# Keys and queries stored as transposed, split columns by the projection stage, in a retention and stick-breaking attention kernel

## The reference, cut to what matters

```python
def shared_kv(x, kv_norm_g, w_kv, sb_k_g):
    kv = rmsnorm(x, kv_norm_g) @ w_kv
    k, v = jnp.split(kv, 2, axis=-1)
    k = rmsnorm(k.reshape(B, L, SB_HEADS, SB_DH), sb_k_g)
    ...
def sb_layer(...):
    q, g = jnp.split(h @ w_in, 2, axis=-1)
    q = rmsnorm(q.reshape(B, L, SB_HEADS, SB_DH), q_g)
    o = stick_breaking(q, k_all, v_all, pos, k_pos, bias).reshape(B, L, SB_W)
    return (jax.nn.silu(g) * o) @ w_out
    ...
# stick_breaking, for query t and key s < t:
#   z[t,s]    = q_t . k_s / sqrt(d) + bias_h
#   A[t,s]    = sigmoid(z[t,s]) * prod_{s<j<t} (1 - sigmoid(z[t,j]))
#   out_t     = sum_s A[t,s] v_s
```

## Time and profile before

| | us |
|---|---|
| runs | 1870.95, 1868.4, 1874.94 |
| median | 1870.95 |
| profiled execution, span | 1868.5 (27997 instructions) |
| retention, up to about | 987 |
| projections of the second layer | 987 to 1352 |
| attention | 1354 to 1760 |
| output product | 1760 to 1868.5 |

### The profile page before, as it was taken

The page is one execution under the profiler, slowest core; times in us unless marked ns, Lnnn a source line. Parts: engine busy times, 40 slices in busy tenths (PEclk is TensorE's granted clock), DMA queues, the critical chain, the costliest instruction groups (busy, mean ns, idle before and its releaser), DMA issues. The chain is left out here.

```text
span 1868.5 us, 27997 instructions
## 1 busy us (share of the span) xinstructions
PE 1801.2 (96%) x10103; PEld 1424.3 (76%) x10103; DVE 1054.1 (56%) x1975; ACT 809.0 (43%) x1682; POOL 81.0 (4%) x140
## 2 busy tenths in 40 slices
PE   4999999999999999999999999999999998999998
PEld 2678787878787878777778777888777777777677
DVE  4653535353635353633656345765168789989752
ACT  3742323232323232412345223533267678989620
POOL 2000000000000000000000000001100000000000
PEclk9999999999999999999999999999999999999999
DMA  9221212131313040583434563212342335554252
GB/s 327 85 94 58 94 58 93 58 94 56 98 52 116 35 128 22 196 275 80 136 79 169 189 217 128 83 67 89 115 113 69 94 94 175 151 150 145 61 176 96
DMA packets 184939, 215.54 MB, mean 115 GB/s; under 512 B 45352, under 2 KB 142560, under 8 KB 183809
## 3 DMA queue, kind: packets, MB, share of 16 engines
q1 hardware_dynamic: 171146, 167.17, 29.2%
q0 software_dynamic: 13696, 47.08, 6.6%
HBM read 165.39 MB, written 48.83 MB: 115 GB/s over the span
## 5 line engine op out<-in xcount | busy, mean ns | idle before, releaser
L475 PE MATMUL rt_acc<-rt_w_hi,rt_h_hi 128*128 128x512 f32 x504 | 203.3, 403 | 1.0 <-DVE rt_h_lo L1017 1.0
L477 PE MATMUL rt_acc<-rt_w_hi,rt_h_lo 128*128 128x512 f32 x504 | 197.1, 391 | 0.0
L476 PE MATMUL rt_acc<-rt_w_lo,rt_h_hi 128*128 128x512 f32 x504 | 196.5, 390 | 0.0
L1060 DVE TENSOR_TENSOR rt_by_cos<-rt_raw,rt_cos 128x256 f32<-128x256 f32 (+1 forms) x72 | 30.5, 424 | 243.8 <-ACT rt_raw L890 243.8
L901 ACT COPY rt_qk_t<-rt_tr 128x256 f32<-128x256 f32 (+1 forms) x72 | 26.0, 361 | 278.6 <-PE rt_tr L709 278.6
L2956 PE MATMUL kq_acc<-kq_w_hi,kq_h 128*128 128x512 f32 x320 | 127.1, 397 | 0.0
L2957 PE MATMUL kq_acc<-kq_w_lo,kq_h 128*128 128x512 f32 x320 | 124.8, 390 | 0.0
L2959 PE MATMUL kq_acc<-kq_w_hi,kq_h 128*128 128x512 f32 x320 | 124.7, 390 | 0.0
L477 PEld LDWEIGHTS rt_acc<-rt_w_hi,rt_h_lo 128*128 128x128 f32 x504 | 94.6, 188 | 20.6
L475 PEld LDWEIGHTS rt_acc<-rt_w_hi,rt_h_hi 128*128 128x128 f32 x504 | 94.9, 188 | 19.2 <-DVE rt_h_lo L1017 1.4
L476 PEld LDWEIGHTS rt_acc<-rt_w_lo,rt_h_hi 128*128 128x128 f32 x504 | 94.9, 188 | 17.9 <-issue 0.2
(11 more groups left out here) (414 smaller groups left out, 4160.1 us busy)
## 6 DMA issues: line engine op xcount, KB each, us to landing
ro_a_raw<-retained SPq DMA_DIRECT2D x14, 1024.0 KB, 5.9
op_ada<-in_ada_w SPq DMA_DIRECT2D x8, 1024.0 KB, 12.8
rt_w_raw<-in_ret_w_in SPq DMA_DIRECT2D x16, 512.0 KB, 5.1
rt_w_raw<-in_ret_w_in SPq DMA_DIRECT2D x8, 1024.0 KB, 7.7
rt_old<-in_state_ret SPq DMA_DIRECT2D x8, 1024.0 KB, 6.0
rt_g_raw<-in_ret_w_in SPq DMA_DIRECT2D x8, 1024.0 KB, 5.2
out_st_sample<-rt_new POOLq DMA_DIRECT2D x8, 1024.0 KB, 8.0
kq_w_raw<-in_sb_w_in SPq DMA_DIRECT2D x4, 2048.0 KB, 8.9
```

The lines of the kernel that those rows point to most:

```text
L475: nc.tensor.matmul(dst, h_hi[:, k, cols], w_hi[:, k, :], start=k == 0, stop=False)
L476: nc.tensor.matmul(dst, h_hi[:, k, cols], w_lo[:, k, :], start=False, stop=False)
L477: last = nc.tensor.matmul(dst, h_lo[:, k, cols], w_hi[:, k, :], start=False, stop=k == KD - 1)
```

## The change

The projection stage transposes the normed rows itself. Behind the product of step s PE turns the four blocks of `kq_out` of step s-1 into a free bank of `kq_tr` (bank 3 in key chunks, bank 1 in query chunks); ACT copies the rounded part and DVE the remainder into `parts` (one buffer, laid over the gate tensor's first half), and POOL stores both, 128 partitions of four runs of 512 bytes each, into new scratch tensors `k_cols` and `q_cols`. Key rows are still stored, as they are outputs; query rows of the prompt are not. Attention loads for each pair both parts of keys and queries for all 1024 positions (`load_heads`, twelve loads of 64 partitions with 4096 bytes each) into buffers of two, and all splits, transposes and copies of keys and queries go from it, with their slots. Sample tiles are treated as before. The page and new-row transposes of the samples take the slots that are free now.

```diff
         self.shift = sb("shift", [P, 3, KD, NC])
+        gate_at = nc.sbuf_base
         self.gate = sb("gate", [NC, 2, D])
+        self.parts = nc.alloc_sbuf_tensor_at("kq_parts", [P, 2, NB // P, P], F32R, offset=gate_at)
         self.cond_t = sb("cond_t", [P, KD, NC])
...
+        self.k_cols = nc.dram_tensor("k_cols", (2, D, SEQ), F32, kind="Internal").ap()
+        self.q_cols = nc.dram_tensor("q_cols", (2, D, SEQ), F32, kind="Internal").ap()
...
-        self.k2 = sb("k2", [P, NPT, 2 * DH])
-        self.k_parts = sb("k_parts", [P, 2, NPT, 2, DH], F32R)
-        self.g_out = sb("g_out", [P, 2, NB])
+        self.k_t = sb("k_t0", [P, 2, SEQ], F32R)
+        self.q_hi = sb("q_hi0", [P, 2, SEQ], F32R)
...
-        self.q4 = sb("q4", [P, 3, 4, 2, 2, DH])
+        self.q_lo = sb("q_lo0", [P, 2, SEQ], F32R)
+        self.g_out = sb("g_out", [P, 2, NB])
...
+HEAD_LOADS = 12
+
+
+def load_heads(sp, ps, pair, k_t, q_hi, q_lo, signal):
+
+    for hh in range(2):
+        cols = slice((2 * pair + hh) * DH, (2 * pair + hh + 1) * DH)
+        for part in range(2):
+            half = slice(part * DH, (part + 1) * DH)
+            sp.dma_start(k_t[half, hh, :].bitcast(F32), ps.k_cols[part, cols, :]).then_inc(signal, 16)
+            sp.dma_start(q_hi[half, hh, :].bitcast(F32), ps.q_cols[0, cols, :]).then_inc(signal, 16)
+            sp.dma_start(q_lo[half, hh, :].bitcast(F32), ps.q_cols[1, cols, :]).then_inc(signal, 16)
 
...
-        k_t = sb("k_t", [P, 2, 2, SEQ], F32R)
-        q_hi = sb("q_hi", [P, 2, 2, QG, P], F32R)
-        q_lo = sb("q_lo", [P, 2, 2, QG, P], F32R)
+        k_t = [pairs.k_t, sb("k_t1", [P, 2, SEQ], F32R)]
+        q_hi = [pairs.q_hi, sb("q_hi1", [P, 2, SEQ], F32R)]
+        q_lo = [pairs.q_lo, sb("q_lo1", [P, 2, SEQ], F32R)]
...
+            def load_pair(pair):
                 if pair >= 2:
-                    sp.wait_ge(k_split, 2 * (pair - 1))
-                src = rows_of["k"][:, :, pair * 2 * DH:(pair + 1) * 2 * DH]
-                sp.dma_start(k2[:], src).then_inc(k_loaded, 16)
-                load_q(2 * pair)
+                    sp.wait_ge(scored, ends[NPT * (pair - 1) - 1] + 1)
+                load_heads(sp, ps, pair, k_t[pair % 2], q_hi[pair % 2], q_lo[pair % 2], heads_loaded[pair % 2])
 
             def load_v(pair):
                 if pair >= 2:
...
-                if at.first and at.u % NPT == 0:
-                    pe.wait_ge(k_taken, 4 * (pair + 1) if pair else 2)
-                if at.first and at.u == NPT // 2:
-                    pe.wait_ge(k_taken, 4)
-                if at.first:
-                    pe.wait_ge(q_lo_s, g + 1)
+                queries = slice(t * P, (t + 1) * P)
+                if pair and at.first and at.u % NPT == 0:
+                    pe.wait_ge(heads_loaded[pair % 2], 16 * HEAD_LOADS * (pair // 2 + pair % 2))
                 own = c0 + n == (t + 1) * P
                 for i, hh in enumerate(at.heads):
-                    dst, keys = z[:, p % 2, i * n:(i + 1) * n], k_t[:, pair % 2, hh, c0:c0 + n]
-                    nc.tensor.matmul(dst, q_hi[:, g % 2, hh, at.u % QG, :], keys, start=True, stop=False)
+                    dst, keys = z[:, p % 2, i * n:(i + 1) * n], k_t[pair % 2][:, hh, c0:c0 + n]
+                    nc.tensor.matmul(dst, q_hi[pair % 2][:, hh, queries], keys, start=True, stop=False)
                     if len(at.heads) == 2:
                         head = 2 * pair + hh
                         nc.tensor.matmul(dst, share[:], bias_parts[:, head:head + 1].to_broadcast([P, n]), start=False, stop=False)
-                    last = nc.tensor.matmul(dst, q_lo[:, g % 2, hh, at.u % QG, :], keys, start=False, stop=not own)
+                    last = nc.tensor.matmul(dst, q_lo[pair % 2][:, hh, queries], keys, start=False, stop=not own)
...
-            turn_k(0, 0)
-            project(0, 2)
-            turn_k(1, 0)
-            project(2, 4)
-            turn_q(0)
-            project(4, 6)
-            turn_k(0, 1)
             score(0)
-            project(6, START)
-            turn_k(1, 1)
+            project(0, START)
             for p in range(NPC):
                 if p + 1 < NPC:
                     score(p + 1)
-                if p in q_slots:
-                    turn_q(q_slots[p])
-                if p in k_slots:
-                    turn_k(*k_slots[p])
...
-            take_k(0, 0)
-            take_k(1, 0)
-            take_q(0)
-            take_k(0, 1)
+            kq_landed(act)
             stick(0)
-            take_k(1, 1)
-            kq_landed(act)
             for p in range(NPC):
                 if p == sample_at[0]:
                     act.wait_ge(sa_ready, 1)
                 if p:
                     stick(p)
-                if p in q_slots:
-                    take_q(q_slots[p])
-                if p in k_slots:
-                    take_k(*k_slots[p])
...
-            rest_q(0)
             kq_landed(dve)
...
+K_CHUNKS, Q_CHUNKS = (1, 2), (4, 5)
+
+
+def rows_stored(s):
+
+    return not (s // NT in Q_CHUNKS and s % NT < NPT)
+
+
+def steps_turned(s):
+
+    return [r for r in range(s) if r // NT in K_CHUNKS + Q_CHUNKS and r % NT < NPT]
+
+
+KQ_STORES = (*(len([r for r in range(n, KQ_STEPS - 1, 2) if rows_stored(r)]) for n in range(2)), 1,
+             2 * len(steps_turned(KQ_STEPS)))
 
 
...
+        def out_free(engine, s):
+
+            if s >= 2:
+                engine.wait_ge(stored[s % 2], last_use(s))
+                if s - 2 in steps_turned(s):
+                    engine.wait_ge(rows_turned, len(steps_turned(s - 1)))
+
+        def turned_at(s):
+
+            return len(steps_turned(s - 1)) if s - 1 in steps_turned(s) else None
+
+        def turned_bank(s):
+
+            return tr[:, 3, :] if s // NT in K_CHUNKS else tr[:, 1, :]
 
...
-            for n in range(2):
-                sp.wait_ge(stored[n], 16 * len(range(n, (SWITCH + 1) * NT, 2)))
+            sp.wait_ge(parts_stored, 32 * len(steps_turned((SWITCH + 1) * NT)))
             sp.dma_start(pairs.far_below[:], t_in["far_below"]).then_inc(consts, 16)
             sp.dma_start(pairs.bias_row[:], t_in["sb_bias"].to_broadcast([P, AH])).then_inc(consts, 16)
-            sp.dma_start(pairs.k2[:], pairs.k_rows(t_out)[:, :, 0:2 * DH]).then_inc(k_loaded, 16)
-            for m in range(2):
-                pairs.load_q(sp, ps, m, q_loaded)
-            sp.wait_ge(q_loaded, 128)
+            load_heads(sp, ps, 0, pairs.k_t, pairs.q_hi, pairs.q_lo, heads_loaded)
+            sp.wait_ge(heads_loaded, 16 * HEAD_LOADS)
             sp.wait_ge(taken, len(steps))
             t = steps[-1][1]
             sp.dma_start(gates_to(t), out[:, (len(steps) - 1) % 2, :]).then_inc(last_stored, 16)
...
+            def turn_rows(s, m):
+                pe.wait_ge(ready, normed_before(s + 1))
+                if m:
+                    pe.wait_ge(parts_lo, m)
+                if s == SWITCH * NT:
+                    pe.wait_ge(full_ready, 2 * NT - proj.EARLY - 1)
+                for d in range(NB // P):
+                    last = nc.tensor.transpose(turned_bank(s)[:, d * P:(d + 1) * P], out[:, s % 2, d * P:(d + 1) * P], ps.ident[:])
+                last.then_inc(rows_turned, 1)
+
...
                 last.then_inc(made, 1)
+                if turned_at(s) is not None:
+                    turn_rows(s - 1, turned_at(s))
                 if c == GATES and t == 0:
                     turn_gates(s - 1)
                 if s == ADA_ADD + 3:
                     pe.wait_ge(mod_ready, 1)
+                    pe.wait_ge(parts_lo, len(steps_turned(s)))
                 for n, i in slots_at(s):
...
+                m = turned_at(s)
+                if m is not None:
+                    act.wait_ge(rows_turned, m + 1)
+                    if m:
+                        act.wait_ge(parts_stored, 32 * m)
+                    nc.scalar.copy(parts[:, 0].rearrange("p d c -> p (d c)"), turned_bank(s - 1)).then_inc(parts_hi, 1)
                 if 3 <= t < 3 + SPLITS and c + 1 < len(chunks):
...
+                m = turned_at(s)
+                if m is not None:
+                    dve.wait_ge(parts_hi, m + 1)
+                    hi, lo = (parts[:, n].rearrange("p d c -> p (d c)") for n in range(2))
+                    nc.vector.tensor_tensor(lo, turned_bank(s - 1), hi.bitcast(F32), ALU.subtract).then_inc(parts_lo, 1)
...
+            def store_parts(s, m):
+                pool.wait_ge(parts_lo, m + 1)
+                c, t = steps[s]
+                half = slice((chunks[c][1] % 2) * NB, (chunks[c][1] % 2 + 1) * NB)
+                for n in range(2):
+                    to = (ps.k_cols if c in K_CHUNKS else ps.q_cols)[n, half, t * P:(t + 1) * P].rearrange("(d p) c -> p d c", p=P)
+                    pool.dma_start(to, parts[:, n].bitcast(F32)).then_inc(parts_stored, 16)
+
             for s, (c, t) in enumerate(steps[:-1]):
                 r = rows(t)
                 _, n, head_gain, _, dst = chunks[c]
                 c0 = (n % 2) * NB
```

(4 more changed lines are left out.)

139 lines of the change are left out of this document (20 added, 119 removed).

## The result

The changed kernel takes 1874.17 us in the median of 20 runs (1871.35 to 1877.46), the kernel before 1870.83 us in 20 runs beside it (1867.87 to 1875.07). The ratio is 1.0017, 95% interval 1.0010 to 1.0023: slower by 3.3 us, less than the 0.3% that I had set as the bound of "same". The forecast was 1858, with 0.17 on "same". The range holds the time; the direction is wrong.

The account below looks back on a forecast made before the run. PE was taken to bound the projection stage and attention's first part, DVE its last. Span 1868.5 - 34.5 (attention) + 21.9 (projection) = 1855.9, plus 2.45 from span to median, gave 1858 us; range 1844 to 1876.

Parts of the forecast that it names:

- the added store loop: Projection stage: ACT's copy waits for the previous tile's two stores; landing taken as 3.9 us, so no stall.
- 32 groups and the sample tiles: Projection stage: 32 transpose groups at 0.44 us cost 14.1 us, the other sample tiles 0.5 us together.
- remainder behind the additions, with the clock: Second key chunk's last prompt tile: DVE's late remainder idles PE 4.9 us, half clock adds 2.4 us.
- start-up of attention: Attention's first block: fifth scoring 6.8 us earlier plus 0.7 us from a kept clock; gain 7.5, bounds 5 and 9.
- rest of attention: Attention after the start-up: removed transposes, copies and splits gain 9, 6 and 12 us in three stretches.
- Bound of the stages: PE limits the projection stage and mainly attention's first part; DVE, with ACT close behind, limits attention's last part.
- Price of a group: Four transposes cost PE 0.35 us until the next matmul starts plus 0.09 in that matmul: 0.44 us.
- Rival C: Attention after the start-up gives only half its price because a scoring-to-transpose chain sets the pace: 1872 us, chance 0.15.
- Rival B: Projection stage: stores landing in 6 us stall query and key chunks, 28 us in all: 1886 us, chance 0.17.
- The forecast stall: Start of the value chunk after the keys: PE idles 4.9 us for DVE's remainder, then half clock costs 2.4 us.
- Edits at nothing: SP's 96 head loads, its wait for the parts, Pool's store order and dropped query-row stores: taken at no cost.
- Runs against the profile: The runs' median lay 2.45 us above the profiled span; this was carried over to the changed kernel.

Follow-up runs that it names:

- e4: Changed kernel with the parts of query tiles in two alternating buffers, each with its own semaphore; 1867.59 us, ratio to before 0.9975.
- e2: Changed kernel with the last chunk's weights, and the constants and heads behind them, loaded only after all part stores landed; 1868.86 us, ratio to before 0.9984.
- e9: Changed kernel with VectorE's remainder ahead of the modulation's additions and two buffers for query tiles' parts; 1859.92 us, ratio to before 0.9939.
- e1: Changed kernel with VectorE's remainder made ahead of the modulation's additions in the second key chunk's last prompt tile; 1868.05 us, ratio to before 0.9977.
- e6: Changed kernel with unread TensorE groups of four transposes put back into attention, waiting for nothing; 1889.81 us, ratio to before 1.0100.
- e11: Changed kernel with each of the projection stage's 32 groups of four transposes made twice in a row; 1881.93 us, ratio to before 1.0057.
- e5: Changed kernel with attention's half alone: only the first key tile is turned, copied and split, stores kept; 1844.27 us, ratio to before 0.9859.
- e3: Changed kernel with only the constants and first pair of heads held until all part stores landed, weights as before; 1872.26 us, ratio to before 1.0009.
- e8: Changed kernel with 59 unread ScalarE copies of 128x512 put back at old slots in attention; 1876.02 us, ratio to before 1.0028.

## Why the prediction was wrong, point by point

The forecast took a gain of 12.6 us from the span and the span became 1.2 us longer. The step that failed first is in the paragraph on the added store loop: "The DMA engines are busy for only 0.24 of 1209:1303, so I take the uncrowded 3.9: no stall". It put the landing of the stores at nothing, and at the two changes of chunk they landed after 8.2 to 8.4 us, behind a load of weights, and cost 6.0 us (e4; the load by e2). The second is the gain of attention: 34.5 us in the sum, 28.3 measured.

The sum was made for one profiled execution: span 1855.9 forecast, 1869.7 measured. Term by term, in us:

| term | forecast | measured | from |
|---|---|---|---|
| 32 groups and the sample tiles | +14.6 | +15.3 | e9: K, V, Q, G |
| remainder behind the additions, with the clock | +7.3 | +6.9 | e1: V |
| landings at the changes of chunk | 0 | +6.0 | e4: Q, G |
| start-up of attention | -7.5 | -5.2 | block's start to fifth scoring |
| rest of attention | -27 | -23.1 | fifth scoring to the end of scoring |
| ahead of the projections and behind attention | 0 | +1.4 | both traces |
| sum | -12.6 | +1.3 | 1.2 between the rounded spans |

- **Bound of the stages.** Right for the projection stage: a group there was paid in full. For attention right up to 1580 and wrong behind it. VectorE's 0.92 of busy time made me give it the last part; with its work put back alone the stretch grows by 5.4, with TensorE's by 9.1 (28 groups for 24). The rule of the Trainium skill (Perfetto Trace Analysis, Identifying the Most-Contended Engine) that was weighed there, to read the weight loads' share and the other engines instead of TensorE's busy time, would have priced this part by VectorE, and e6 speaks against it here.
- **Price of a group.** 0.44 in key tiles, as forecast, and 0.49 in query tiles, 0.05 more in each of 16; why is open, since the second four in e11 cost 0.44 there too. Its lower bound of 0.35, the way to the next matmul's start, was no bound (e11).
- **Rest of attention.** The three stretches were to gain 9, 6 and 12 us; A1, A2 and A3 gained 5.8, 5.9 and 10.4, and another 1.1 came between the fifth scoring and A1. The term that was mis-sized is the first, "22 x 0.44 = 9.7 us of PE", taken as 9. TensorE's busy time fell by 8.5 us in A1, but its idle time rose from 3.4 to 6.1: part of what was removed had filled waits. VectorE's 12.3 in the last part was too much as well: 17 instructions fewer took 9.5 us off its busy time, 0.56 each and not 0.69, because queued instructions overlap in the traces: the changed kernel's subtraction at 1163.34 takes 0.69 us, and VectorE's next instruction starts 0.61 us after it. A removed instruction was worth its distance to the next start, not its duration. Rival C named this mechanism (a chain sets the pace) and had its size too large: it took half of the price away, where 14% was lost (23.1 of 27).
- **Start-up.** From the same block start the fifth scoring was to come at 10.3 us and came at 12.0. The 0.7 us that were taken from "A PE that isn't idle keeps its clock" did not come. TensorE has no wait of 3.88 us any more, but now the clock is at half behind the 2.94 us of the change of blocks: 0.86 in these 12 us, the first matmuls 0.63 us each. Before, the same change of blocks, an idle of 2.93 us, had no such fall behind it. The fall moved and did not go.
- **The store loop.** L was 3.9, as taken, and in plain tiles it cost nothing. What failed is the sentence from which it was taken: "The DMA engines are busy for only 0.24 of 1209:1303". That is a mean over 94 us, and the store that matters is issued 0.12 us behind a load of 2 MB that takes 9.5 us. The loop at the change to the gates was never laid out, and behind it stood a short sample tile, where TensorE has little work to hide a wait. Rival B's mechanism thus came true at the changes of chunk alone, by another cause than it gave; its L of 6 us in every tile was not there. The Trainium skill's fit (DMA: Bandwidth & Descriptors, Anatomy of one DMA — SWDGE (gpsimd) path) gave an estimated 3.2 us for both stores and, by the same working, gives an estimated 2.6 for one of 256 KB. Here one such store landed in 3.1 in the median and the pair in 3.9 from the first issue, so these stores were slower than the fit, while the 2.3 us of plain stores lay below it rather than on it.
- **The forecast stall.** Right in place, length (4.62 against 4.9), releaser and clock (2.3 us behind it against 2.4). That it was seen and priced before it existed is the part of the method that worked; the same walk through the gate chunk would have found the other one.
- **Edits at nothing.** SyncE's 96 head loads and Pool's order cost nothing that the changed kernel shows; the 1.3 us in e5's K go with the stores of the parts. The head loads land in 8 to 9 us in the median, and the value loads in 8.2 where it was 4.9, inside a lead of a whole pair.
- **Runs against the profile.** I carried 2.45 us from span to median for both kernels. The profiled execution of the changed kernel is the fastest of its 20, 2.8 us under its median, so the true difference is 3.3 us and not 1.2; the granted clock over the whole span was 0.992 in it and 0.987 in the mean of its runs.

Without the two stalls that order and buffers make (e9), the change gives 1859.9, near the forecast's 1858. That is half a coincidence, since the forecast had one of these stalls in it and too much gain in attention.

## What to carry to other kernels

Lay out every in-order queue at every irregular step (the last tile of a chunk, a short tile, the place where a side job is added up), not for the regular tile alone: all 13 us of stalls here lay in three such steps, and an order of two instructions and a second buffer took them away. Ask of a transfer what is issued in the microsecond before it, not how busy the DMA engines are on average. An instruction taken from an engine gives back its distance to the next start, less the idle time that it covered: TensorE's groups, put back alone, cost 58% (A1) and 74% (A3) of their 0.44 us here, and VectorE's subtractions on top of them nothing and 1.7 us. Prices of engines in one chain do not add.

## What was not expected of the hardware

The granted clock falls at places that shift between nearly equal programs. The changed kernel and e1 have the same instructions there and the same idle of 0.96 us in front of a scoring near 1412, with one of 0.74 us right behind it; only e1 has a lower clock around them. TensorE's timeline in the changed kernel, then in e1:

```profile
1414.01 0.41 PE L1690 MATMUL z<-pa_k_t,pa_q_hi 128*128 128x384 f32 x1 [0.96 <-ACT pa_take L1847]
```

```profile
1412.49 0.41 PE L1690 MATMUL z<-pa_k_t,pa_q_hi 128*128 128x384 f32 x1 [0.96 <-ACT pa_take L1847]
```

The stretches around it (granted clock in the third column from the end), of the changed kernel and of e1; the first pair begins 1.0 us ahead of that scoring, the second 2.4 us:

```profile
1412.98:1417.98 5.00, 3.30 (x28) 2.58 (x28) 4.82 (x7) 3.07 (x6) 0.54 (x1) 1.00 0.15 56
1417.98:1422.98 5.00, 5.00 (x33) 3.88 (x33) 4.69 (x7) 3.97 (x8) 0.00 (x0) 1.00 0.00 0
```

```profile
1410.13:1415.13 5.00, 3.30 (x19) 2.25 (x20) 3.77 (x5) 3.92 (x7) 0.54 (x1) 0.86 0.14 52
1415.13:1420.13 5.00, 5.00 (x38) 3.93 (x37) 4.78 (x7) 2.42 (x6) 0.00 (x0) 0.80 0.01 3
```

Each such fall costs about 1.5 us, as the column A1 shows: 121.85 in the changed kernel, e3 and e8, 123.4 in e4, e5 and e9, 124.9 in e1, e2 and e11, with the same TensorE work. The second 1.5 us of e1 and e2 are the fall near 1412, the first a like one about 100 us later. The clock is also most of what one kernel's runs differ by: by a straight line through 31 runs of the kernel before (each with its span's mean clock, 0.988 to 0.994), 0.001 less of it goes with 1.05 us more, and through the 20 of the changed kernel with 0.85. What decides whether such an idle of 1 us brings the clock down stays open; no run here varied it alone.
